# Hybrid diffusion trunk on one core: expert weights streamed on two issuing queues in place of one

## The reference, cut to what matters

```
def expert_choice_ffn(x, p):
    B, L, D = x.shape
    cap = CAPACITY_FACTOR * L // N_EXPERTS
    aff = jax.nn.softmax((x @ p['w_router']).astype(jnp.float32), axis=-1)
    g, idx = lax.top_k(jnp.swapaxes(aff, 1, 2), cap)
    xs = x[bidx, idx]
    h = (jax.nn.silu(jnp.einsum('becd,edf->becf', xs, p['w_gate']))
         * jnp.einsum('becd,edf->becf', xs, p['w_up']))
    y = jnp.einsum('becf,efd->becd', h, p['w_down']) * g[..., None].astype(x.dtype)
    return jnp.zeros_like(x).at[bidx, idx].add(y)
```

## Time and profile before

| | us |
|---|---|
| median of 3 runs (2309.58 to 2316.5) | 2312.7 |
| profiled execution | 2314.85 |
| its span, first to last instruction | 2313.0 |

### The profile page before, as it was taken

The page is one execution under the profiler, slowest core; times in us unless marked ns, Lnnn a source line. Parts: engine busy times, 40 slices in busy tenths (PEclk is TensorE's granted clock), DMA queues, the critical chain, the costliest instruction groups (busy, mean ns, idle before and its releaser), DMA issues.

```text
span 2313.0 us, 59357 instructions
## 1 busy us (share of the span) xinstructions
PE 2164.6 (94%) x25462; PEld 1489.2 (64%) x25462; DVE 857.1 (37%) x2104; ACT 540.0 (23%) x1389; POOL 636.4 (28%) x635
## 2 busy tenths in 40 slices
PE   5999999999999999999997599999999999999998
PEld 3468888777777777544443476666666666766664
DVE  4124442366767767555625212222222111122201
ACT  3001111144554545434426400000000000000000
POOL 0245773255554555356623000000000000000000
PEclk9999999999999999999999799999999999999999
DMA  9932231354454443876622699999999999999996
GB/s 368 384 99 56 70 82 60 87 151 134 141 148 132 132 143 115 315 262 214 214 96 104 260 352 411 414 415 415 414 414 415 421 412 408 407 414 402 413 408 251
DMA packets 184211, 610.11 MB, mean 264 GB/s; under 512 B 16670, under 2 KB 93176, under 8 KB 156172
## 3 DMA queue, kind: packets, MB, share of 16 engines
q1 hardware_dynamic: 151672, 552.52, 61.9%
q10 hardware_dynamic: 30644, 43.31, 6.0%
q0 software_dynamic: 1632, 10.49, 2.3%
HBM read 587.07 MB, written 19.20 MB: 262 GB/s over the span
## 4 chain that ended last, share of the span: by engine, by line
PE 72%; DMA 18%; DVE 3%; ACT 2%; issue 2%; SPq 1%; ACTq 1%; POOL 1%; DVEq 0%; POOLq 0%
PE PS L1990 18%; PE PS L1643 14%; PE PS L2004 10%; DMA work<-in_w_gate 8%; PE PS L1465 8%; PE PS L1785 7%; DMA mixT_<-in_w_gate 3%; PE PS L1407 3%; DMA work<-in_w_ada 3%; DMA hT_<-in_w_gate 2%; PE PS L1342 2%; PE PS L1637 2%; PE PS L1369 1%; PE PS L2030 1%; PE PS L1608 1%
## 5 line engine op out<-in xcount | busy, mean ns | idle before, releaser
L1990 PEld LDWEIGHTS PS<-hT_,work 128*64 128x64 f32 x11904 | 425.6, 140 | 123.5 <-issue 67.2
L1990 PE MATMUL PS<-hT_,work 128*64 128x80 f32 x11904 | 441.3, 235 | 56.3 <-DMA work<-in_w_gate 21.7
L2746 POOL TENSOR_TENSOR work<-work 128x512 f32<-128x512 f32 x240 | 320.9, 1337 | 285.8 <-ACT work L1109 275.4
L1785 PE MATMUL PS<-work,mixT_ 128*128 128x512 f32 x640 | 285.4, 600 | 0.0
L2811 POOL DMA_INDIRECT out_y<-mixT_,work x15 | 21.5, 1434 | 814.2 <-DVE mixT_ L2623 814.2
L1323 ACT ACTIVATE hT_<-PS 128x480 f32<-128x480 f32 x16 | 9.1, 571 | 912.5 <-PE PS L1990 912.5
L1643 PE MATMUL PS<-hT_,work 128*128 128x320 f32 x768 | 221.4, 434 | 0.0
L1465 PE MATMUL PS<-work,hT_ 128*128 128x256 f32 x960 | 214.5, 382 | 2.2 <-DMA work<-in_w_in 2.2
L1785 PEld LDWEIGHTS PS<-work,mixT_ 128*128 128x128 f32 x640 | 119.7, 192 | 144.4 <-issue 144.3
L1109 ACT ACTIVATE work<-work,cT 128x512 f32<-128x512 f32 x256 | 174.6, 716 | 130.2 <-DMA work<-in_w_ada 61.5
L1465 PEld LDWEIGHTS PS<-work,hT_ 128*128 128x128 f32 x960 | 181.2, 191 | 28.4 <-DMA work<-in_w_in 3.0
(11 more groups left out here) (334 smaller groups left out, 2451.5 us busy)
## 6 DMA issues: line engine op xcount, KB each, us to landing
work<-in_w_gate SPq DMA_DIRECT2D x47, 2048.0 KB, 22.2
work<-in_w_up SPq DMA_DIRECT2D x46, 2048.0 KB, 27.2
work<-in_w_down SPq DMA_DIRECT2D x45, 2048.0 KB, 27.7
work<-in_w_in SPq DMA_DIRECT2D x80, 512.0 KB, 5.2
work<-in_w_ada SPq DMA_DIRECT2D x147, 256.0 KB, 2.8
work<-in_w_ada SPq DMA_DIRECT2D x16, 2048.0 KB, 18.7
work<-in_w_ada ACTq DMA_DIRECT2D x109, 256.0 KB, 3.3
mixT_<-in_w_up SPq DMA_DIRECT2D x10, 2048.0 KB
```

The source lines that it names most:

```text
L1785: last = pe.matmul(bank(tt), mix_at(k)[:, tt * P:(tt + 1) * P], w_out_ring[(2 * n + k // 8) % 3][:, k % 8, :], start=(k == 0), stop=(k == ...
L1990: last = pe.matmul(hidden_at(u, f)[64 * h:64 * h + 64, :], w[:, k % 4, f // 2, f % 2, 64 * h:64 * h + 64], xsT[s][:, k, :], start=opens, s ...
L2746: TT_(acc_ctx[p % 3], acc_ctx[p % 3], prod[i % 2], ALU.add).then_inc(s_padd, 1)
```

## The change

Up pieces from r = 7 on are no longer issued by SP. SP's loop passes over them; its other pieces, their waits and their order stay. ScalarE issues the up pieces on its own queue, into the same slots and with the same semaphores. Before `hidden(e)` it issues those whose slot comes free while TensorE computes expert e, each after the same wait on `s_used` as before.

```
+        def up_weights(r):
+
+            return r >= RING and piece_of(r)[1] in (1, 3, 5, 7)
...
             for r in range(RING, 12 * EXPERTS):
-                sp.wait_ge(s_used, START + used_up_to(r - RING))
-                piece(*piece_of(r), r)
+                if not up_weights(r):
+                    sp.wait_ge(s_used, START + used_up_to(r - RING))
+                    piece(*piece_of(r), r)
...
+            def up_piece(r):
+
+                e, j = piece_of(r)
+                act.dma_start(w_ring[r % RING], w_up_v[:, e:e + 1, j // 2:j // 2 + 1].rearrange("p e b i n -> p (e b) (i n)"))\
+                    .then_inc(s_w[r % RING], 16)
...
+            ups = [r for r in range(12 * EXPERTS) if up_weights(r)]
             for e in range(EXPERTS):
+                for r in ups:
+                    if (done_gate_up(e - 1) if e else 0) < used_up_to(r - RING) <= done_gate_up(e):
+                        act.wait_ge(s_used, START + used_up_to(r - RING))
+                        up_piece(r)
                 hidden(e)
                 if e + 2 < EXPERTS:
                     gathered(e + 2)
```

## The result

The changed kernel takes 2316.75 us (median of 16 runs, 2312.03 to 2324.7) against 2311.49 us (16 runs, 2306.85 to 2318.8). The ratio is 1.0024, with a 95% interval of 1.0013 to 1.0036: slower by 5.5 us, between 3.0 and 8.3 (the medians differ by 5.3). The forecast was +6.8 us. The interval leaves out 0, but the loss is 0.24%, under the 0.3% that the prediction took as the least that can be told from no change.

The account below looks back on a forecast made before the run. The weight stream was taken as the bound, through gate 182's landing. Landing order +9.5 and earlier issue -2.7 gave +6.8 us, on a median of 2312.7: 2319.5, stated as 2320, range 2304 to 2334 us.

Parts of the forecast that it names:

- What bounds it: Expert phase: weight stream at 62.9 us an expert against TensorE's 58.3; landing of gate 182 sets the end.
- Issue cost 0: ScalarE's queue: issuing the up pieces delays neither an up nor the hidden step, cost 0.
- Earlier issue, -2.7: Start of the expert phase: ups issued 2.7 us earlier into idle DMA time, kept to the end, -2.7 us.
- Order of landing, +9.1 to +9.8: Last expert: ups 183 and 186 overtake gate 182, which lands 1.85 to 2 pieces later, +9.1 to +9.8 us.
- The stream does not starve, 0: While gate 182 is awaited, 182, 184, 185 and 187 are still in flight, 20 us of stream.
- Clock: TensorE's granted clock: more concentrated waits may add dips; 0, at most +1 us at the end.
- What would show it: Ups landing in 10 to 14 us, last awaited gate some 7 us later, the same 52.8 us behind it.
- the 1% that was named as a sign of being wrong: Weights' rate from 1440 to 2280 us stays near 400 GB/s; a move of over 1% means wrong.
- 1: Rival: the stream's end decides, landing order does not matter, early 2.7 us kept, 2310 us; chance 0.22.
- 2: Rival: two interleaved weight streams run slower, 2328 us at 1% of rate, 2340 at 413 GB/s; chance 0.2.
- 3: Rival: two streams fill gaps of one, faster, 2301 us at 2% more rate; chance 0.11.
- 4: Rival: ScalarE blocks on an up wait or issues an up late, at most 1 us slower; 0.02 with others.

Follow-up runs that it names:

- e7: Kernel before, with only up pieces 183 and 186 of the last expert issued by ScalarE: +9.7 us against the kernel before.
- e8: Kernel before, with only up piece 186 issued by ScalarE: +4.6 us against the kernel before.
- e1: Changed kernel, but ScalarE issues up pieces only from 7 to 151 and SP all pieces from 152 on: -1.2 us against the kernel before.
- e6: Kernel before, one queue, with pieces 17 and 18, and 20 and 21, changing places: -0.5 us against the kernel before.
- e2: Changed kernel, but SP issues all pieces below 152 and ScalarE the up pieces only from 152 on: +9.0 us against the kernel before.
- e5: Kernel before, one queue, SP issuing all pieces from 7 on in the order their slots come free: +2.5 us against the kernel before.
- f3: Kernel before, one queue, pieces 7 to 67 issued in the order their slots come free: -0.7 us against the kernel before.
- f1: Kernel before, with GpSimd's scatter of expert 13 held until TensorE finished gate 185: +0.2 us against the kernel before.

## Why the prediction was right

*What bounds it*: right. Gates are what TensorE waits for; e7 and e8 show the end move with gate 182 piece for piece. But TensorE is nearer to being the bound than the prediction has it. It is 93% busy in the phase (949.0 of 1016.1 us), not 98%, and the 58.3 us an expert leave out its other waits. In e1, where it set the end alone, it took 184.0 us for three experts (gate 146 begun at 2065.41, gate 182 at 2249.39), 61.3 each, with 1.7 us of it from a lower clock at gate 146. Against the stream's 62.9 its room is some 2 us an expert and not 4.6, and a gate that lands early can give no more than that.

*Issue cost 0*: right. In expert 1 TensorE ended j = 7 at 1390.11 in the chain and ScalarE's hidden step began at 1390.16; ScalarE issues took 0.33 us.

*Earlier issue, -2.7*: the mechanism is there. ScalarE issued up piece 18 at 1353.35 (timeline), as soon as its product ended, 4.73 us after expert 1's j = 2 began in TensorE's chain at 1348.62 (before: 1359.59 and 1367.32, 7.73 us), and of the two half-idle windows of the earlier trace rows one is left. Windows of the kernel after:

```profile
1350.00:1356.00 6.00, 6.00 (x122) 3.85 (x117) 0.00 (x0) 0.00 (x0) 0.00 (x0) 1.00 0.72 265
1356.00:1362.00 6.00, 6.00 (x146) 5.27 (x146) 0.00 (x0) 0.00 (x0) 0.00 (x0) 1.00 1.01 429
```

The lead was 2.7 us after 143 us. I had put it on the first early piece alone; e6 shows that the first two are not enough. The term's step from there to the end, that a lead in a saturated stream is kept, did not hold with two queues: it was gone after 743 us. That e2 and e7, without the lead, cost 9.0 and 9.7 and the changed kernel 5.5 would fit a lead that is kept, but the intervals overlap.

*Order of landing, +9.1 to +9.8*: right where nothing else interferes (e7: gate 182 9.0 us later). In the changed kernel it was 2.9 MB, 6.8 us, at gate 170, so mis-sized there. That both ups are fully ahead was right, 2.0 pieces. What the sum left out is that pieces behind the awaited gate move before it has landed in the one queue as well, 1.9 of them at gate 170. Only the difference counts, and of those on SP's queue 1.25 were left: 2.0 + 1.25 - 1.9 = 1.4 pieces.

*The stream does not starve, 0*: wrong in this profile, with a size that is not firm. Weights in the phase from 343 to 543 us, first before (1639.94 to 1839.94), then after (1629.29 to 1829.29):

```profile
q1 hardware_dynamic: 5534, 80.61, 95.0%
```

```profile
q1 hardware_dynamic: 3632, 52.82, 62.2%
q10 hardware_dynamic: 1779, 25.97, 31.8%
```

That is 1.8 MB less; from 543 to 743 us it is 0.5 MB more, in sum 1.3 MB or 3.1 us. In windows of 5 us over these 400 us, those with a DMA share under 0.98 add up to 3.7 us of idle engines in the changed kernel and 0.6 before; in e1, which has the same two queues there, to 1.8 (and 0.6 MB less than before), on one queue in e5 to 1.2 and in f3 to 0.6. So the engines were idle 1 to 3 us longer with two queues. By bytes the size is less firm still, since the profiles with one queue in this stretch spread from 159.3 to 160.3 MB (before 159.9, e1 159.3, changed 158.5). One such stretch lies behind a wait of TensorE for a gate that landed at 1802.97:

```profile
1800.00:1820.00 20.00, 16.99 (x326) 12.69 (x328) 0.00 (x0) 0.00 (x0) 0.00 (x0) 0.91 0.95 395
```

The likely reason, argued and not tested, is that with ups landed and unused fewer pieces are under way, and when TensorE waits none is issued. At gate 170 no issue stands in either queue between 2177.09 and 2190.88, and the engines then fell idle (behind the stretch counted above). Window of the kernel after:

```profile
2180.00:2200.00 20.00, 16.11 (x300) 12.59 (x304) 0.00 (x0) 0.00 (x0) 0.00 (x0) 0.83 0.93 387
```

The three terms add up to the later landing of gate 170: 6.8 - 2.7 + 3.1 = 7.2 us, measured 7.1. That is bookkeeping of the bytes in the same two profiles and no second proof. So two errors of about 3 us, one in each direction, cancel: that the forecast of +6.8 came so near is in part luck. The mechanism, ups ahead of an awaited gate, is not.

*Clock*: too low. The same window shows 0.83; gate 170's products took 6.95 us for 4.65, 2.3 us, where I had said at most +1. With 2.3 us of issue waits behind it that is most of what TensorE took above 58.3 us from gate 170 to gate 182, 64.4 us. It came too late to wait for gate 182. Before, it took 63.3 us, a wait for gate 182 among them.

*What would show it*: landings of ups 15.2 us (said 10 to 14), gates and downs 1.5 and 4.6 us sooner (said as before or longer), last awaited gate 7.1 us later (said 7), but one expert earlier and not with 52.8 us behind it. The weights' rate from 1440 to 2280 us is 396 GB/s (332.85 MB), 0.9% less, just inside the 1% that was named as a sign of being wrong.

*Rivals*: 1 is ruled out by e7 and e8. 2 finds no support: in e1, with two queues for most of the phase, nothing is lost, where a rate 1% lower would cost over 7 us; a rate lower by some tenths of a percent is not excluded. 3 falls with the sign. 4: the rows of expert 1 show no late up and no blocked step.

## What to carry to other kernels

When a stream is consumed in a fixed order and its landing sets the end, put all of it on one queue: here a second one shared the bandwidth, and what came early on it made the awaited piece late. Such a loss falls due once, at the last awaited piece, so test by changing only the last few transfers; one transfer in 192 was enough here. Count the bytes of each queue when the awaited piece lands: they say what really went ahead of it, and how much did so already before the change. Count every consumer behind the awaited piece before moving traffic away from it (f1), and compare profiles from the start of the phase when the part before it varies by more than the effect.
